# A hybrid decoder block on one core: transposed operands of the two attention groups built by VectorE and a trip through DRAM instead of by TensorE

## The chip, the cores and the metric

The kernel runs on one core of one Trainium2 chip. The metric is the device time of one execution in microseconds (us); three runs were made. Besides them there is one profiled execution, from which all rows below come. A core has five engines with queues of their own: TensorE (PE, matmuls, results go to PSUM), VectorE (DVE), ScalarE (ACT), GpSimd (POOL) and SyncE (SP), which here issues nearly all DMAs. Engines wait for each other through semaphores, and each engine works through its instructions strictly in the order in which they are written.

## The reference

256 tokens of 1024 numbers pass through one block. After an RMS norm, a projection `h @ w_in` gives the parts of two head groups.

```python
b = cumsum(log_a) in chunks of 64            # GLA: gated linear attention, 4 heads, dk 64, dv 128
q_dec, k_inv = q * exp(b), k * exp(-b)
a = where(causal, q_dec @ k_inv.T, 0)        # per head
o = a @ v + q_dec @ state                    # state carried over the chunks
# MoBA: 4 heads of 128; 256 tokens are one block, so it is plain causal attention
p = softmax(rotary(mq) @ rotary(mk).T * dh**-0.5, causal)
o_moba = p @ mv
```

Each head's output is RMS-normed (GLA also gated by silu(gr)), both groups go through `w_out` onto the residual x, and a SwiGLU of width 2816 and a last norm follow. All is float32.

## The kernel before

Every float32 product with a weight is built from three matmuls: weights and activations are split into a rounded high part and the low rest, and hi x hi, hi x lo and lo x hi are summed in PSUM (`product`, L471 to L473). Weights come in units of 128x2048 numbers (1 MB). SP loads unit u into one of three `raw` buffers when VectorE is done with unit u-3 (`raw_free`). ScalarE casts it to `w_hi` (`split`, L858), VectorE subtracts to get `w_lo` (its `split`, L1072), and six buffers of both feed TensorE. Units 0 to 11 are w_in in blocks of 512 columns, two units a block, in the order gla q and k, moba q, moba k, moba v, gla v, gla gate; units 12 to 15 are w_out; then eleven FFN phases of three units each. ScalarE takes a finished block out of PSUM with `take_block(b, ...)` (L875).

The small steps of the two attention groups are put between these units by hand. On TensorE the tables `midway` (after a unit's first token tile) and `after` (behind a unit) say where; on the other engines the order of the program does it. The steps touched are:

- GLA: VectorE scales q and k by the decays (L1180 to L1185). `gla_transposed`, behind unit 4, turns ten 128x128 tiles by matmuls with the identity (L576); ScalarE and VectorE copy them into `qdT`, `kiT`, `qcT`. `gla_scores` (L626) stands behind unit 6. `qdT` holds the query rows of the two heads of a pair apart; each scores matmul uses the 64 rows of one head.
- MoBA: `rotate(0)` and `rotate(1)` on VectorE (L1170 to L1175) apply the rotary embedding to queries and keys. `moba_transposed(0)`, behind unit 6, and `moba_transposed(1)`, in the middle of unit 7, turn eight tiles each; copies go to `mT` (L935, L940 on ScalarE, L1194, L1208 on VectorE). `moba_scores` (L636, L640) stands behind unit 7. VectorE adds the mask and takes the row maxima (L1212 to L1222), ScalarE the exponentials (L948). `probs_transposed`, in the middle of unit 9, turns twelve tiles, copied out by L955 and L1227. `moba_outputs` (L658) and `gla_updates` (L670) stand in the middle of unit 10; in the middle of unit 11 stand `heads_transposed(0)` and then `gla_outputs` (L682, L685).

The transposes of VectorE itself work in blocks of 32x32 inside a group of 32 partitions. The FFN phases already use them: sixteen instructions of 32x128 numbers per phase (L1321).

Of the kernel before, what the change touches and what calls it, by code (L numbers as in the profile page):

```python
# [22 lines left out]
P = 128  # L23
SEQ, D = 256, 1024
T = SEQ // P
KC = D // P
HEADS = 4
DV = 128
DK = 64
# [25 lines left out]
QUADS = 4  # L55
# [34 lines left out]
def build_block(nc, x, positions, norm1_gain, w_in, w_gate_up, b_gate, gla_out_gain, moba_out_gain,  # L90
# [6 lines left out]
    with ExitStack() as ctx:  # L97
# [83 lines left out]
        k_end, q_cum = (reuse_c[:, 1024 + QK * i:1024 + QK * (i + 1)] for i in range(2))  # L181
# [11 lines left out]
        mT = reuse_f[:, :].rearrange("p (w h s) -> p w h s", w=2, h=HEADS)  # L193
# [60 lines left out]
        glaT_in_psum = sem("glaT_in_psum")  # L254
        glaT_by_act = sem("glaT_by_act")
        glaT_by_dve = sem("glaT_by_dve")
        mT_in_psum = sem("mT_in_psum")
        mT_by_act = sem("mT_by_act")
        mT_by_dve = sem("mT_by_dve")
# [42 lines left out]
        out1_right_ready = sem("out1_right_ready")  # L302

# [4 lines left out]
        def _(sp):  # L308
# [84 lines left out]
        def _(pool):  # L393
# [14 lines left out]
            nc.gpsimd.memset(qdT[:, :, :, :], 0.0)  # L408
# [58 lines left out]
        def _(pe):  # L467
# [118 lines left out]
            def cumulate():  # L586
# [5 lines left out]
                for t, tri in enumerate((tri_rest, tri_cum)):  # L592
                    cols = slice(t * QK, (t + 1) * QK)
                    nc.tensor.matmul(aux[:, 3, cols], tri[:, :], log_hi[:, cols], start=True, stop=False)
                    last = nc.tensor.matmul(aux[:, 3, cols], tri[:, :], log_lo[:, cols], start=False, stop=True)
                last.then_inc(cum_in_psum, 1)

            def gla_transposed():
                pe.wait_ge(gla_ops_ready, 3)
                for bank, src in ((1, q_mid), (2, k_mid)):  # L600
                    transposes(bank, [src[:, t, pair * P:(pair + 1) * P] for pair in range(PAIRS)
                                      for t in range(T)]).then_inc(glaT_in_psum, 1)
                transposes(0, [q_cum[:, pair * P:(pair + 1) * P] for pair in range(PAIRS)]).then_inc(glaT_in_psum, 1)

            def moba_transposed(which):
                pe.wait_ge(rotated, which + 1)
                if which == 0:
                    pe.wait_ge(glaT_by_act, 3)
                else:
                    pe.wait_ge(mT_by_act, 1)  # L610
                    pe.wait_ge(mT_by_dve, 1)
                for n, bank in enumerate((3, 0)):
                    transposes(bank, [m_rot[:, which, t, h, :] for h in (2 * n, 2 * n + 1)
                                      for t in range(T)]).then_inc(mT_in_psum, 1)

            def gla_scores():

                pe.wait_ge(glaT_by_act, 2)
                pe.wait_ge(glaT_by_dve, 1)
                for t in range(T):  # L620
                    tok = slice(t * P, (t + 1) * P)
                    for pair in range(PAIRS):
                        col = (t * PAIRS + pair) * P
                        for par in range(2):
                            rows = slice(par * DK, (par + 1) * DK)
                            last = nc.tensor.matmul(aux[:, 1 + par, col:col + P], kiT[rows, pair, tok],  # L626
                                                    qdT[rows, pair, par, tok], start=True, stop=True)
# [782 lines left out]
```

## Time and profile before

| | us |
|---|---|
| median of 3 runs | 305.72 (305.68 to 305.84) |
| the profiled execution's own time | 305.38 |
| its span, first to last instruction | 303.7 |
| TensorE busy in it | 296.2 |
| VectorE busy | 231.7 |
| ScalarE busy | 153.7 |
| GpSimd busy | 21.9 |

The span is what the trace covers; the device time holds 1.7 us more around it. "Busy" sums the instructions of an engine. A matmul's duration is longer than its distance to the next one, since they are pipelined, so costs on TensorE are read from start to start. The granted clock is given as a share of full speed, the DMA share as the mean share of the core's 16 DMA engines that were moving data.

### The profile page before, as it was taken

The numbers are of one execution on the slowest core, as the hardware profiler recorded it, in microseconds if no ns is written. First come the engines' busy times: TensorE is split into PE (matmuls) and PEld (weight loads), VectorE is DVE, ScalarE is ACT, GpSimd is POOL, SyncE is SP. The second block draws the span as 40 slices with busy tenths as digits, with TensorE's granted clock in tenths as the row PEclk, the third lists the DMA queues.
The fourth block names the chain that finished last, engine by engine and source line by source line (L and its number), as shares of the span: only waits on it lengthen the run. The fifth ranks groups of instructions, "written<-read, shape, count | busy, mean of one in ns | idle before, by whom it ended". The sixth has DMA issues, their size and how long they took to land.

```text
span 303.7 us, 4006 instructions
## 1 busy us (share of the span) xinstructions
PE 296.2 (98%) x1407; PEld 247.1 (81%) x1407; DVE 231.7 (76%) x375; ACT 153.7 (51%) x189; POOL 21.9 (7%) x42
## 2 busy tenths in 40 slices
PE   8999999999999999999999999999999999999992
PEld 7788888888888888888888888888888888888881
DVE  1999999996487257679797979797878878787155
ACT  2898994699363527326262626262617071713123
POOL 6050100000112001500000000000000000000011
PEclk9999999999999999999999999999999999999998
DMA  7987856337825303914747474747472919030003
GB/s 233 359 294 254 276 200 218 138 141 276 276 86 192 138 2 92 316 77 156 262 158 259 159 255 158 256 163 252 139 276 82 331 34 368 19 133 0 0 2 138
DMA packets 36599, 54.42 MB, mean 179 GB/s; under 512 B 2870, under 2 KB 25962, under 8 KB 36586
## 3 DMA queue, kind: packets, MB, share of 16 engines
q1 hardware_dynamic: 36420, 54.08, 52.1%
q8 instruction: 8, 0.13, 0.2%
q10 hardware_dynamic: 166, 0.17, 0.2%
q14 instruction: 5, 0.04, 0.0%
HBM read 53.19 MB, written 1.05 MB: 179 GB/s over the span
## 4 chain that ended last, share of the span: by engine, by line
PE 94%; DMA 2%; DVE 1%; issue 1%; POOL 1%; ACT 0%; SPq 0%; POOLq 0%; DVEq 0%
PE acc L471 15%; PE acc L473 14%; PE acc L472 14%; PE aux L471 13%; PE aux L472 13%; PE aux L473 13%; PE aux L576 3%; DMA raw<-in_w_in 2%; PE acc L525 1%; PE acc L528 1%; PE acc L531 1%; PE aux L658 1%; DVE x_sb L1285 1%; PE aux L682 1%; PE aux L640 1%
## 5 line engine op out<-in xcount | busy, mean ns | idle before, releaser
L1072 DVE TENSOR_TENSOR w_lo<-raw,w_hi 128x2048 fp32r<-128x2048 f32 x47 | 105.6, 2287 | 11.3 <-ACT w_hi L858 11.2
L858 ACT CAST w_hi<-raw 128x2048 fp32r<-128x2048 f32 x47 | 87.7, 1907 | 6.9 <-DMA raw<-in_w_out 3.3
L471 PE MATMUL aux<-w_hi,aT_hi 128*128 128x512 f32 (+1 forms) x180 | 69.8, 388 | 0.0
L473 PE MATMUL aux<-w_hi,aT_lo 128*128 128x512 f32 (+1 forms) x180 | 69.6, 387 | 0.0
L472 PE MATMUL aux<-w_lo,aT_hi 128*128 128x512 f32 (+1 forms) x180 | 69.6, 387 | 0.0
L1321 DVE STREAM_TRANSPOSE reuse_c<-reuse_c 32x128 f32<-32x128 f32 x160 | 48.4, 303 | 2.4
L471 PE MATMUL acc<-w_hi,aT_hi 128*128 128x512 f32 x118 | 47.3, 401 | 0.0
L473 PE MATMUL acc<-w_hi,aT_lo 128*128 128x512 f32 x118 | 46.1, 391 | 0.0
L472 PE MATMUL acc<-w_lo,aT_hi 128*128 128x512 f32 x118 | 46.0, 390 | 0.0
L473 PEld LDWEIGHTS aux<-w_hi,aT_lo 128*128 128x128 f32 x180 | 33.8, 188 | 6.9
L471 PEld LDWEIGHTS aux<-w_hi,aT_hi 128*128 128x128 f32 x180 | 33.8, 188 | 6.9
L472 PEld LDWEIGHTS aux<-w_lo,aT_hi 128*128 128x128 f32 x180 | 33.8, 188 | 6.7
L1015 ACT CAST pT_hi<-reuse_c 128x512 fp32r<-128x512 f32 x10 | 6.2, 621 | 64.7 <-DVE reuse_c L1321 64.7
L471 PE MATMUL acc<-w_hi,pT_hi 128*128 128x512 f32 x80 | 31.2, 390 | 0.0
L473 PE MATMUL acc<-w_hi,pT_lo 128*128 128x512 f32 x80 | 31.1, 389 | 0.0
L472 PE MATMUL acc<-w_lo,pT_hi 128*128 128x512 f32 x80 | 31.1, 389 | 0.0
L1002 ACT ACTIVATE reuse_c<-aux,rstd 128x256 f32<-128x256 f32 x22 | 10.2, 472 | 32.4 <-PE aux L473 32.3
L473 PEld LDWEIGHTS acc<-w_hi,aT_lo 128*128 128x128 f32 x118 | 22.2, 188 | 4.8
L471 PEld LDWEIGHTS acc<-w_hi,aT_hi 128*128 128x128 f32 x118 | 22.2, 188 | 4.4 <-issue 0.2
L472 PEld LDWEIGHTS acc<-w_lo,aT_hi 128*128 128x128 f32 x118 | 22.2, 188 | 4.3
L1311 DVE SCALAR_TENSOR_TENSOR reuse_c<-aux,rstd,reuse_c 128x256 f32<-128x256 f32 x22 | 10.2, 480 | 13.2 <-ACT reuse_c L1002 13.2
L473 PEld LDWEIGHTS acc<-w_hi,pT_lo 128*128 128x128 f32 x80 | 15.0, 188 | 3.2
(199 smaller groups left out, 272.1 us busy)
## 6 DMA issues: line engine op xcount, KB each, us to landing
raw<-in_w_ffn_gate SPq DMA_DIRECT2D x22, 512.0 KB, 4.2
raw<-in_w_ffn_up SPq DMA_DIRECT2D x22, 512.0 KB, 5.3
raw<-in_w_ffn_down SPq DMA_DIRECT2D x22, 512.0 KB, 5.7
raw<-in_w_in SPq DMA_DIRECT2D x20, 512.0 KB, 4.7
raw<-in_w_out SPq DMA_DIRECT2D x8, 512.0 KB, 3.9
raw<-in_w_in SPq DMA_DIRECT2D x8, 256.0 KB, 6.2
x_sb<-in_x SPq DMA_DIRECT2D x2, 512.0 KB, 3.9
reuse_a<-in_final_norm_gain SPq DMA_DIRECT2D x1, 512.0 KB, 4.3
```

Source lines behind the costliest of these rows:

```text
L471: nc.tensor.matmul(dst, left_hi[:, k, tok], right_hi, start=first, stop=False)
L472: nc.tensor.matmul(dst, left_hi[:, k, tok], right_lo, start=False, stop=False)
L473: return nc.tensor.matmul(dst, left_lo[:, k, tok], right_hi, start=False, stop=last)
L525: nc.tensor.matmul(acc[:, t, :], aT_hi[:, k, toks[t]], right_hi, start=k == 0, stop=False)
L528: nc.tensor.matmul(acc[:, t, :], aT_hi[:, k, toks[t]], right_lo, start=False, stop=False)
L576: last = nc.tensor.transpose(aux[:, bank, n * P:(n + 1) * P], src, ident[:, :])
L858: nc.scalar.copy(w_hi[:, slot % RING, :], raw[:, slot % RAW, :]).then_inc(hi_ready, 1)
L1002: nc.scalar.activation(silu_g[:, t, :], aux[:, GATE_UP_BANKS[parity][t], 0:FF], ACT.Silu, scale=rstd[:, 1, t:t + 1]).then_inc(silu_ready, 1)
L1015: nc.scalar.copy(dst, src.rearrange("p (k s) -> p k s", k=2)).then_inc(hiddenT_hi_ready, 1)
L1072: nc.vector.tensor_tensor(w_lo[:, slot % RING, :], raw[:, slot % RAW, :], w_hi[:, slot % RING, :].bitcast(f32), ALU.subtract).then_inc(lo_ ...
L1311: nc.vector.scalar_tensor_tensor(out=hidden[:, t, :], in0=aux[:, GATE_UP_BANKS[parity][t], FF:2 * FF], scalar=rstd[:, 1, t:t + 1], in1=sil ...
L1321: last = nc.vector.transpose(cols[SQUARE * c:SQUARE * (c + 1), :, :, g, :], rows[SQUARE * g:SQUARE * (g + 1), :, :, c, :])
```

## The change

The ten GLA tiles and the sixteen MoBA tiles no longer pass through TensorE. VectorE turns all 32x32 blocks of a set of tiles in one wide instruction (`gla_squares`: 128x1280; `m_squares`: 128x1024 for the queries, the same for the keys). SP then stores each result in a DRAM scratch tensor (`squares_out`, one DMA) and reads it back so that every block lands in the right group of 32 partitions (`columns_back`, four DMAs of 32 partitions, after a wait until the store is done). ScalarE copies those parts that serve as stationary operands into a contiguous form (`kT`, 768 columns; `mT_q`, 1024 columns); the others are read by the matmuls as they land.

Moved with it: `moba_scores` from behind unit 7 to behind unit 8, `probs_transposed` from the middle of unit 9 to behind it, `gla_outputs` ahead of `heads_transposed(0)` and ScalarE's squares ahead of its copies of the head outputs. On ScalarE, split(9) goes behind take_block(2), split(12) behind the exponentials, take_block(3) ahead of split(11). On VectorE, rotate(1) goes ahead of split(8), split(9) behind the masked copies of the GLA scores, split(12) behind the copy of the probabilities. `q_cum` and `k_end` and the two halves of the PSUM bank of their decays change places, so that the ten tiles lie side by side. The memset of `qdT` goes.

```diff
-        qdT = sb("qdT", [PAIRS, 2, SEQ])
-        kiT = sb("kiT", [PAIRS, SEQ])
-        qcT = sb("qcT", [PAIRS, P])
+        gla_columns = sb("gla_columns", [QUADS, GLA_TILES, SQUARE])
+        kT = sb("kT", [3 * PAIRS, P])
...
+        gla_moves = nc.dram_tensor("gla_moves", (P, QUADS, GLA_TILES * SQUARE), f32).ap()
+        m_moves = [nc.dram_tensor(f"m_moves_{w}", (P, QUADS, MOBA_TILES * SQUARE), f32).ap() for w in "qk"]
...
-            for u in range(RAW, IN_UNITS):
-                raw_free(u)
-                rows_unit(u % RAW, w_in[0], (u % 2) * 4 * P, 4, BLOCKS[u // 2], 512)
+            def squares_out(ready, n, moves, squares, moved):
+                sp.wait_ge(ready, n)
+                sp.dma_start(moves, squares.rearrange("p c n i -> p c (n i)")).then_inc(moved, 16)
+
+            def columns_back(moved, moves, columns, landed):
+                sp.wait_ge(moved, 16)
+                for c in range(QUADS):
+                    sp.dma_start(columns[SQUARE * c:SQUARE * (c + 1)].rearrange("p g n i -> p g (n i)"),
+                                 moves[:, c, :].rearrange("(g j) n -> j g n", g=QUADS)).then_inc(landed, 16)
+
+            in_units(RAW, 9)
+            squares_out(gla_squares_ready, 1, gla_moves, gla_squares, gla_moved_out)
+            in_units(9, 10)
+            columns_back(gla_moved_out, gla_moves, gla_columns, gla_columns_back)
+            in_units(10, 11)
+            squares_out(m_squares_ready, 1, m_moves[0], m_squares[0], m_moved_out[0])
+            columns_back(m_moved_out[0], m_moves[0], m_columns[0], m_columns_back[0])
+            squares_out(m_squares_ready, 2, m_moves[1], m_squares[1], m_moved_out[1])
+            in_units(11, IN_UNITS)
+            columns_back(m_moved_out[1], m_moves[1], m_columns[1], m_columns_back[1])
...
             def gla_scores():
-                pe.wait_ge(glaT_by_act, 2)
-                pe.wait_ge(glaT_by_dve, 1)
+                pe.wait_ge(gla_columns_back, 16 * QUADS)
+                pe.wait_ge(kT_ready, 1)
...
             def moba_scores():
-                pe.wait_ge(mT_by_act, 2)
-                pe.wait_ge(mT_by_dve, 2)
+                pe.wait_ge(mT_q_ready, 1)
+                pe.wait_ge(m_columns_back[1], 16 * QUADS)
                 pe.wait_ge(a_ready, 2)
...
-            midway = {2: [logits], 7: [lambda: moba_transposed(1)],
-                      9: [probs_transposed], 10: [moba_outputs, gla_updates], 11: [lambda: heads_transposed(0, (3, 0)), gla_outputs]}
-            after = {3: [cumulate], 4: [gla_transposed],
-                     6: [gla_scores, lambda: moba_transposed(0)], 7: [moba_scores]}
+            midway = {2: [logits], 10: [moba_outputs, gla_updates], 11: [gla_outputs, lambda: heads_transposed(0, (3, 0))]}
+            after = {3: [cumulate], 6: [gla_scores], 8: [moba_scores], 9: [probs_transposed]}
...
             split(8)
-            act.wait_ge(glaT_in_psum, 1)
-            nc.scalar.copy(qdT[0:DK, :, 0, :], ...).then_inc(glaT_by_act, 1)
-            act.wait_ge(glaT_in_psum, 2)
-            nc.scalar.copy(kiT[:, :, :], ...).then_inc(glaT_by_act, 1)
-            act.wait_ge(glaT_in_psum, 3)
-            nc.scalar.copy(qcT[:, :, :], ...).then_inc(glaT_by_act, 1)
-            split(9)
             act.wait_ge(rotated, 1)
             take_block(2, m_flat)
-            act.wait_ge(mT_in_psum, 1)
-            nc.scalar.copy(mT[:, 0, 0:2, :], ...).then_inc(mT_by_act, 1)
+            split(9)
+            act.wait_ge(gla_columns_back, 16 * QUADS)
+            nc.scalar.copy(kT[...], gla_columns[...]).then_inc(kT_ready, 1)
             split(10)
+            act.wait_ge(m_columns_back[0], 16 * QUADS)
+            nc.scalar.copy(mT_q[...], m_columns[0][...]).then_inc(mT_q_ready, 1)
+            act.wait_ge(rotated, 2)
+            take_block(3, mv)
             split(11)
-            act.wait_ge(rotated, 2)
-            act.wait_ge(mT_in_psum, 3)
-            nc.scalar.copy(mT[:, 1, 0:2, :], ...).then_inc(mT_by_act, 1)
-            split(12)
-            take_block(3, mv)
...
             nc.scalar.preload_act_table(ACT.Silu)
+            split(12)
             split(13)
...
+            dve.wait_ge(gla_ops_ready, 3)
+            nc.vector.transpose(gla_squares, gla_rows).then_inc(gla_squares_ready, 1)
             split(6)
             split(7)
-            rotate(0)
+            for which in range(2):
+                rotate(which)
+                dve.wait_ge(rotated, which + 1)
+                nc.vector.transpose(m_squares[which], m_rows[:, which]).then_inc(m_squares_ready, 1)
             split(8)
-            dve.wait_ge(glaT_in_psum, 1)
-            nc.vector.tensor_copy(qdT[DK:P, :, 1, :], ...).then_inc(glaT_by_dve, 1)
-            rotate(1)
-            dve.wait_ge(mT_in_psum, 2)
-            nc.vector.tensor_copy(mT[:, 0, 2:4, :], ...).then_inc(mT_by_dve, 1)
-            split(9)
...
                 last.then_inc(a_ready, 1)
-            dve.wait_ge(mT_in_psum, 4)
-            nc.vector.tensor_copy(mT[:, 1, 2:4, :], ...).then_inc(mT_by_dve, 1)
+            split(9)
             split(10)
```

## Rows read from the trace of the kernel before

**Rows 1.** The page: busy us, share of the span, instructions; the chain that ended last.

```profile
PE 296.2 (98%) x1407; PEld 247.1 (81%) x1407; DVE 231.7 (76%) x375; ACT 153.7 (51%) x189; POOL 21.9 (7%) x42
...
PE 94%; DMA 2%; DVE 1%; issue 1%; POOL 1%; ACT 0%; SPq 0%; POOLq 0%; DVEq 0%
```

**Rows 2.** Stretches: busy us per engine (instructions), granted clock, DMA share, GB/s.

```profile
34.00:52.00 18.00, 18.00 (x90) 14.81 (x90) 17.36 (x24) 14.19 (x18) 0.96 (x1) 1.00 0.65 218
52.00:63.00 11.00, 11.00 (x72) 9.58 (x70) 10.11 (x14) 6.29 (x5) 0.00 (x0) 1.00 0.43 154
63.00:81.00 18.00, 18.00 (x105) 15.30 (x103) 11.86 (x10) 13.42 (x29) 0.00 (x0) 1.00 0.67 243
```

**Rows 3.** TensorE in order of time: start, duration, instruction; a run of one kind merged.

```profile
39.50 1.25 PE L576 MATMUL aux<-ident,reuse_c 128*128 128x128 f32 x10
40.51 0.48 PE L471 MATMUL acc<-w_hi,aT_hi 128*128 128x512 f32 x1
...
46.06 0.39 PE L471 MATMUL acc<-w_hi,aT_hi 128*128 128x512 f32 x1
...
51.27 0.39 PE L473 MATMUL acc<-w_hi,aT_lo 128*128 128x512 f32 x1
...
52.69 1.09 PE L576 MATMUL aux<-ident,reuse_e 128*128 128x128 f32 x8
53.53 0.48 PE L471 MATMUL acc<-w_hi,aT_hi 128*128 128x512 f32 x1
...
56.40 1.04 PE L576 MATMUL aux<-ident,reuse_e 128*128 128x128 f32 x8
57.19 0.48 PE L471 MATMUL acc<-w_hi,aT_hi 128*128 128x512 f32 x1
```

**Rows 4.** The same view: MoBA scores, the product behind them, MoBA outputs.

```profile
60.01 1.05 PE L636 MATMUL aux<-reuse_f 128*128 128x128 f32 x8
...
62.44 0.58 PE L471 MATMUL acc<-w_hi,aT_hi 128*128 128x512 f32 x1
...
77.61 2.84 PE L658 MATMUL aux<-mv,reuse_f 128*128 128x128 f32 x24
```

**Rows 5.** VectorE: a group of the page (busy, mean ns); then in order of time.

```profile
L1321 DVE STREAM_TRANSPOSE reuse_c<-reuse_c 32x128 f32<-32x128 f32 x160 | 48.4, 303 | 2.4
...
37.76 4.49 DVE L1072 TENSOR_TENSOR w_lo<-raw,w_hi 128x2048 fp32r<-128x2048 f32 x2
42.18 0.69 DVE L1170 TENSOR_TENSOR reuse_e<-reuse_d,cos_t 128x512 f32<-128x512 f32 x1
...
45.57 0.69 DVE L1175 TENSOR_TENSOR reuse_e<-reuse_e,mv 128x512 f32<-128x512 f32 x1
...
65.19 0.17 DVE L1222 TENSOR_SCALAR neg_max<-row_max 128x4 f32<-128x4 f32 x1
```

**Rows 6.** ScalarE in order of time; in brackets idle time before and what ended it.

```profile
47.40 1.26 ACT L875 ACTIVATE reuse_d<-acc,rstd 128x512 f32<-128x512 f32 x2
...
67.36 0.51 ACT L948 ACTIVATE reuse_e<-reuse_e,neg_max 128x256 f32<-128x256 f32 x1
67.77 0.19 ACT L948 ACTIVATION_READ_ACCUMULATOR reuse_e<-reuse_e,neg_max 128x1 f32 x1
...
69.27 1.91 ACT L858 CAST w_hi<-raw 128x2048 fp32r<-128x2048 f32 x1
71.47 1.08 ACT L955 COPY reuse_f<-aux 128x512 f32<-128x512 f32 x2 [0.29 <-PE aux L576]
```

**Rows 7.** DMA issues: count, KB, us from issue to landing; then SP's queue in time.

```profile
raw<-in_w_ffn_gate SPq DMA_DIRECT2D x22, 512.0 KB, 4.2
...
out<-reuse_e SPq DMA_DIRECT2D x2, 256.0 KB, 2.2
...
40.08 0.88 SPq L320 DMA_DIRECT2D raw<-in_w_in  x2
```

**Rows 8.** Stretch at the end, TensorE: busy us, granted clock, DMA share, GB/s.

```profile
290.00:303.70 13.70, 7.69 (x40) 0.93 0.21 78
```

More of the change, by code:

```diff
@@ L180, in build_block @@
         q_mid, k_mid = (reuse_c[:, 512 * i:512 * i + 512].rearrange("p (t n) -> p t n", t=T) for i in range(2))
-        k_end, q_cum = (reuse_c[:, 1024 + QK * i:1024 + QK * (i + 1)] for i in range(2))
+        q_cum, k_end = (reuse_c[:, 1024 + QK * i:1024 + QK * (i + 1)] for i in range(2))
+        gla_rows = reuse_c[:, 0:GLA_TILES * P].rearrange("p (n c i) -> p c n i", c=QUADS, i=SQUARE)
+        gla_squares = reuse_f[:, 0:GLA_TILES * P].rearrange("p (c n i) -> p c n i", c=QUADS, i=SQUARE)
         squares = reuse_c[:, 0:1024]
@@ L192, in build_block @@
         s_1 = reuse_e[:, 512:1536].rearrange("p (h k) -> p h k", h=HEADS)
-        mT = reuse_f[:, :].rearrange("p (w h s) -> p w h s", w=2, h=HEADS)
+        m_columns = [reuse_f[:, 1024 * w:1024 * (w + 1)].rearrange("p (c n i) -> p c n i", c=QUADS, i=SQUARE) for w in range(2)]
+        mT_q = reuse_a[:, :].rearrange("p (t h s) -> p t h s", t=T, h=HEADS)
+        mT_k = reuse_f[:, 1024:2048].rearrange("p (c t h i) -> p t h c i", c=QUADS, t=T, h=HEADS)
+        m_rows = reuse_e[:, :].rearrange("p (w n c i) -> p w c n i", w=2, c=QUADS, i=SQUARE)
+        m_squares = [buf.rearrange("p (c n i) -> p c n i", c=QUADS, i=SQUARE)
+                     for buf in (reuse_a[:, :], reuse_c[:, 0:1024])]
         probT = reuse_f[:, 0:1536].rearrange("p (b h q) -> p b h q", b=3, h=HEADS)
@@ L253, in build_block @@
         gla_ops_ready = sem("gla_ops_ready")
[L254 to L259, printed above, removed]
+        gla_squares_ready = sem("gla_squares_ready")
+        gla_moved_out = sem("gla_moved_out")
+        gla_columns_back = sem("gla_columns_back")
+        kT_ready = sem("kT_ready")
+        m_squares_ready = sem("m_squares_ready")
+        m_moved_out = [sem(f"m_moved_out_{w}") for w in "qk"]
+        m_columns_back = [sem(f"m_columns_back_{w}") for w in "qk"]
+        mT_q_ready = sem("mT_q_ready")
         a_zeroed = sem("a_zeroed")
@@ L592, in cumulate @@
                 for t, tri in enumerate((tri_rest, tri_cum)):
-                    cols = slice(t * QK, (t + 1) * QK)
-                    nc.tensor.matmul(aux[:, 3, cols], tri[:, :], log_hi[:, cols], start=True, stop=False)
-                    last = nc.tensor.matmul(aux[:, 3, cols], tri[:, :], log_lo[:, cols], start=False, stop=True)
+                    cols, dst = slice(t * QK, (t + 1) * QK), slice((1 - t) * QK, (2 - t) * QK)
+                    nc.tensor.matmul(aux[:, 3, dst], tri[:, :], log_hi[:, cols], start=True, stop=False)
+                    last = nc.tensor.matmul(aux[:, 3, dst], tri[:, :], log_lo[:, cols], start=False, stop=True)
                 last.then_inc(cum_in_psum, 1)
[L598 to L614, printed above, removed]
             def gla_scores():
-                pe.wait_ge(glaT_by_act, 2)
-                pe.wait_ge(glaT_by_dve, 1)
+                pe.wait_ge(gla_columns_back, 16 * QUADS)
+                pe.wait_ge(kT_ready, 1)
                 for t in range(T):
-                    tok = slice(t * P, (t + 1) * P)
                     for pair in range(PAIRS):
@@ L639, in moba_scores @@
                 for h in range(HEADS):
-                    last = nc.tensor.matmul(aux[:, 2 + h // 2, (h % 2) * SEQ:(h % 2 + 1) * SEQ], mT[:, 0, h, P:SEQ],
-                                            mT[:, 1, h, :], start=True, stop=True)
+                    last = nc.tensor.matmul(aux[:, 2 + h // 2, (h % 2) * SEQ:(h % 2 + 1) * SEQ], mT_q[:, 1, h, :],
+                                            mT_k[:, :, h, :, :], start=True, stop=True)
                     if h % 2:
```

34 lines of the change are left out of this document (18 added, 16 removed).

## The prediction

> **What bounds the kernel now.** I read the page first: TensorE is busy for 98% of the span and is 94% of the chain that ended last [rows 1]. Next I read busy time by stretch: from 34 to 81 us, where most of the change lies, TensorE has no free time at all and its clock is at full speed; up to 63 us VectorE is close behind it, with 17.4 of 18 and 10.1 of 11 us [rows 2]. So the kernel is a queue of matmuls. What leaves this queue is gained in full, and what makes it wait is lost in full. The third view was TensorE in order of time [rows 3, 4], then the other engines at the points where the new order ties TensorE to them [rows 5 to 7].
>
> **What is removed.** Three groups of transposes leave TensorE. By starts, the ten GLA transposes take 39.50 to 40.51 us, and the product behind them lasts 0.48 instead of 0.39 us: 1.01 + 0.09 = 1.1 us. The query group takes 52.69 to 53.53, 0.84 us; the slow restart behind it stays, since the GLA scores now stand there. The key group takes 56.40 to 57.19, and with its restart 0.88 us [rows 3]. Sum: **-2.85 us**, an upper bound of the gain. The copies of their results out of PSUM leave ScalarE and VectorE; those engines are followed below.
>
> **First wait, GLA scores.** A unit of weights is 24 products, from 46.06 to 51.27 + 0.23 = 5.44 us [rows 3]. Without the ten transposes units 5 and 6 end at 39.50 + 10.9 = 50.4, and the scores now need a ScalarE copy (kT_ready). Its chain: VectorE's added transpose of 1280 columns. One of 128 columns takes 0.303 us, a 128x512 pass 0.69, so 128 more columns cost about 0.13, and 1280 cost 0.303 + 9 x 0.13 = 1.5 us, of which some 0.07 overlaps its neighbour. It stands before split(6), so the first rotation, ready at 45.57 + 0.69 = 46.26 before, is ready at 47.7 [rows 5]. The profile shows no such wide transpose. Lower bound 0.83 us (a pass with one source at twice the speed), upper bound 2 us (ten at 0.303 less overlaps); I take 1.45, since both rows it lies between run at this rate. Behind the rotation ScalarE runs take_block(2), 1.26, split(9), 1.91 [rows 6], and the kT copy of 768 columns, about 0.8 (half as much again as a 512-column copy at 0.54). Less overlaps of 0.1 each that is 51.7. TensorE waits 51.7 - 50.4 = **1.3 us**. Behind the waiting scores stands everything else on TensorE. The other input, the moved columns, is not later by my estimate: VectorE is done at 39.2, the store lands near 43.2, the return is issued from 43.2 to 45.0 behind unit 9 and lands near 49 (bounds 47.5 and 51).
>
> **The moves.** Nothing in the trace goes through DRAM and back. The nearest rows: a 256 KB store lands 2.2 us after issue, a 512 KB load of 1 KB rows 4.2 us, an issue costs 0.44 us on SP [rows 7]. So I take about 3.4 us for each store of 512 or 640 KB and, for four returns issued 0.45 apart, 4.2 us from the first issue. The stretch 34 to 52 moved 218 GB/s at a DMA share of 0.65, so about 330 GB/s when busy [rows 2]; a weight unit of 1 MB then holds the engines 3.1 us. SP's queue in order: unit 9 at 41.5, GLA return 43.2, unit 10 at 45.0, query store when VectorE has turned them. That is 47.7 + 1.24 = 49.0 and behind unit 10's bytes, landed 53.7; query return issued to 55.5, landed 57.9. The keys are turned at 54.4 (second rotation 4.1 us, then 1.24), but SP is free only at 55.5; their store lands at 59.4. Unit 11 goes in between, at 56.7, when split(8) is done, and the key return, issued from 59.4, has its bytes behind it: it lands at **64.6**. Bounds: 61.8 if no transfer is held by another, 67.4 if each return needs a further 1 to 1.5 us and every queue delay falls on this chain.
> Every unit behind keeps its slack: split(8) at 56.7 against TensorE's unit 8 at 58.4, split(9) at 60.2 against 66, split(10) at 62.4 against 74.
>
> **Second wait, scores.** After the first wait GLA scores take 1.2 us and units 7 and 8 10.9, so TensorE comes to the MoBA scores at 63.8. The wait is 64.6 - 63.8 = **0.8 us**, bounds 0 and 3.6. Call the start of these scores S; before it was 60.01 [rows 4].
>
> **Third wait, MoBA outputs.** Before, with S = 60.01, the second maxima end at 65.19 + 0.17 = S + 5.35, the exponentials at 67.77 + 0.19 = S + 7.95, after take_block(3) had held the first four back; without this, four of 0.41 + 0.19 us, each overlapped by 0.1, behind the maxima give S + 7.4 [rows 5, 6]. TensorE: scores 2.43, a unit 5.44 and restarts, so the probability transposes start at S + 8.05: not late, by 0.6 us only. They take 1.3 (twelve at 0.10, as in rows 3, and a restart), half a unit 2.72: TensorE wants the transposed probabilities at S + 12.1. ScalarE has a table load until S + 8.75 (1.3, from 67.96 to 69.27), then split(12) and split(13), 1.83 each, where only one stood before, then two copies, 1.08 [rows 6]: S + 13.5. Wait **1.4 us**. Then the outputs, 2.77 [rows 4], to S + 16.3, while split(14) and take_block(4) end at S + 16.5: **0.2 us** more for the GLA updates. If those two splits stood behind the copies, 1.4 would be nothing.
>
> **The rest.** After these steps TensorE stands at the middle of unit 11 at S + 22.7. The swap of GLA outputs and head transposes puts ScalarE's squares before its copies; headsT is ready about 4.1 us after this point, wanted at 6.3: hidden. The later order of split(12) on VectorE is hidden by more than 10 us of lead. The memset of qdT that GpSimd drops, the swapped halves of the decay bank and the new shapes of the score operands (same count and columns) I put at nothing: bounds +-0.1. Four restarts out of a wait, of some 0.07 each: **0.3 us** (bounds 0 and 0.6).
>
> **Sum:** -2.85 + 1.3 + 0.8 + 1.4 + 0.2 + 0.3 = **+1.15 us**. The profiled execution took 305.38 us for its span of 303.7, which is 0.34 below the median of 305.72; 305.38 + 1.15 = 306.5 would be its like, and against the median the forecast is **306.9 us**.
>
> **A rule weighed.** The key return's chain rests on row 7's 2.2 us for 256 KB. The Trainium skill, "DMA: Bandwidth & Descriptors", section on the anatomy of one DMA, gives about 2.0 us fixed plus bytes over 436 GB/s, most of the fixed part being the receipt of the write, heaviest for HBM; the 2.2 us is a little below its 2.6. By it alone store and return would be about 3.2 us each and the key columns would be there before S, an estimate that leaves out the weights in front. The sum would be about 0.8 lower. It is the first rival's case.
>
> **Rivals.** (1) *No DMA wait*: the key columns land by 63.8. For it: the bound of 61.8, and a DMA share of 0.43 from 52 to 63 us [rows 2]. Against: SP, in order, holds unit 11 between. The sum is then +0.35, 306.1. (2) *The move chain is the bound*: the key columns land at 66 to 67.4, or the GLA columns later than ScalarE. For it: two round trips in series on one queue and 3.4 MB on top of the weights. The key wait is 2.2 to 3.6, the time 308.3 to 309.7. (3) *Faster*: VectorE's wide transposes run like a pass with one source, 0.83 and 0.68 us. Then the rotation comes 0.65 earlier, the first wait is 0.65, the key chain gains more than 1 us and its wait goes; with restarts at nothing -2.85 + 0.65 + 1.6 = -0.6, 305.1. It decides at a wide transpose of 0.9 us or less. Against: 303 ns for 128 columns. (4) *The clock falls*: TensorE now has idle gaps of 1 us or more close together. In the last stretch, where it is idle for 6.0 of 13.7 us, the granted clock shows 0.93, in the stretches without idle time 1.00 [rows 2, 8]. If it fell to the lower level of 1.2 GHz after the third wait, half a unit of 2.7 us would take 5.4: +3 to +5 us on the sum, 309.9 to 311.9.
> The Trainium skill, "TensorE: Matmul & The Clock Gate", says that an engine that has been idle is put back to half clock until it has again been busy; whether the gaps forecast here would do it, nothing in the trace shows.
>
> **How the numbers follow.** Forecast, key wait between 0.3 and 2: 0.45. (1) 0.25, (2) 0.16, (3) 0.10, (4) 0.04. What a measurement can tell from no change is about 0.2%, 0.6 us. Slower by more: nearly all of the forecast's case, (2), (4) and a little of (1): 0.66. Within: 0.24. Faster: 0.10. The range 305.2 to 309.3 leaves out half of (3), a part of (2) and (4); the forecast's own is 306.3 to 308.2.
>
> **What would show it.** TensorE's list has no 128x128 products out of ident between 39 and 57 us; the GLA scores wait about 1.3 us for ScalarE's kT; the MoBA scores wait for a DMA by about 0.8; the MoBA outputs wait about 1.4 us for ScalarE's copy of the probabilities. A wide transpose lasts 1.5 and 1.24 us. The stretches behind 110 us are unchanged. I am wrong if TensorE meets the MoBA outputs without a wait, or if a store or return lands more than 1.5 us away from the times given.

## The result and the profile after

| | before | after |
|---|---|---|
| median of 4 runs, us | 305.78 (305.68 to 306.10) | 309.12 (308.48 to 311.54) |
| ratio to before | | 1.0131, 95% interval 1.0101 to 1.0162 |
| the profiled execution's own time, its span | 305.38, 303.7 | 311.54, 309.8 |

The changed kernel is 1.3% slower: +3.34 us in the medians, against +1.15 in the forecast. The direction was right and the time lies at the upper end of the range, among the times of rival (2), though the keys landed later than that rival has them. The profiled execution of after is the slowest of its four, so it shows +6.1 us of span; the experiments below hold a second profile of the same kernel with +5.0. No profile shows an execution at the median, so there the waits below must be shorter than in either.

The page of after: busy us, share and instructions; the chain that ended last; then its DMA issues with the median us to landing.

```profile
PE 296.0 (96%) x1381; PEld 246.5 (80%) x1381; DVE 233.9 (76%) x375; ACT 153.1 (49%) x186; POOL 21.1 (7%) x41
...
PE 82%; ACT 5%; DVE 5%; issue 3%; DMA 2%; SPq 1%; POOL 1%; POOLq 0%; DVEq 0%; ACTq 0%
...
gla_columns<-gla_moves SPq DMA_DIRECT2D x4, 160.0 KB, 6.0
m_moves_q<-reuse_a SPq DMA_DIRECT2D x1, 512.0 KB, 6.0
...
m_moves_k<-reuse_c SPq DMA_DIRECT2D x1, 512.0 KB, 3.7
reuse_f<-m_moves_k SPq DMA_DIRECT2D x4, 128.0 KB, 4.0
```

TensorE issues 26 matmuls fewer and yet is busy for about as long as before [rows 1]: about half of what the transposes cost has gone into slower score matmuls, 1.44 us as shown below. Its share of the chain fell from 94% to 82%; the other engines and DMA now stand in it. TensorE in order of time at the three places where it waits (start, duration, in brackets the idle time ahead of it and what ended it); these answer to [rows 3, 4]. The first row is the last product ahead of the GLA scores:

```profile
50.52 0.39 PE L507 MATMUL acc<-w_hi,aT_lo 128*128 128x512 f32 x1
52.63 1.16 PE L642 MATMUL aux<-gla_columns,kT 64*128 64x128 f32 x16 [1.73 <-ACT kT L943]
...
69.00 2.05 PE L652 MATMUL aux<-reuse_f,reuse_a 128*128 128x128 f32 x8 [4.10 <-issue]
...
72.87 0.58 PE L505 MATMUL acc<-w_hi,aT_hi 128*128 128x512 f32 x1
...
83.56 2.94 PE L674 MATMUL aux<-mv,reuse_f 128*128 128x128 f32 x24 [0.77 <-ACT reuse_f L965]
```

The books of this execution, by starts: -2.85 (transposes) + 1.79 (first wait: the scores start 2.11 behind the last product, before 0.32) + 4.25 (MoBA scores wait for the keys) + 1.44 (these scores take 3.87 instead of 2.43) + 0.92 (wait at the outputs) + 0.20 (the outputs themselves take 2.97 instead of 2.77) + 0.38, by which the whole queue stands later already at the cumulate step, ahead of the change (33.47 against 33.09). That makes 6.13, and the spans differ by 6.1. Nothing later adds to it. Stretches (busy us per engine, granted clock, DMA share, GB/s):

```profile
58.00:62.00 4.00, 4.00 (x19) 3.33 (x18) 4.00 (x3) 2.21 (x3) 0.00 (x0) 1.00 1.03 338
62.00:66.00 4.00, 2.91 (x13) 2.06 (x11) 0.58 (x1) 0.00 (x0) 0.00 (x0) 1.00 1.10 266
66.00:70.00 4.00, 1.00 (x5) 1.03 (x6) 0.00 (x0) 1.90 (x1) 0.00 (x0) 0.80 1.02 376
70.00:74.00 4.00, 4.00 (x18) 3.49 (x18) 2.81 (x6) 1.26 (x7) 0.00 (x0) 0.77 0.24 96
```

Two things stand here that before did not have: from 58 to 70 us the DMA engines have no free time (shares of 1.0 and above; before, 0.43 from 52 to 63 [rows 2]), and the clock falls in the stretches at 66 and 70, behind the long gap. SP's queue (start, us spent issuing) says what stands in front of what; ScalarE and VectorE below say when the data came:

```profile
42.76 2.09 SPq L383 DMA_DIRECT2D gla_columns<-gla_moves  x4
44.90 0.94 SPq L333 DMA_DIRECT2D raw<-in_w_in  x2
...
55.30 1.75 SPq L383 DMA_DIRECT2D reuse_f<-m_moves_q  x4
57.09 0.43 SPq L378 DMA_DIRECT2D m_moves_k<-reuse_c  x1
57.57 1.35 SPq L333 DMA_DIRECT2D raw<-in_w_in  x2
60.84 1.75 SPq L383 DMA_DIRECT2D reuse_f<-m_moves_k  x4
```

ScalarE, with what ended its idle time in brackets:

```profile
51.66 0.83 ACT L943 COPY kT<-gla_columns 128x768 f32<-128x768 f32 x1 [0.57 <-DMA gla_columns<-gla_moves]
54.04 1.92 ACT L872 CAST w_hi<-raw 128x2048 fp32r<-128x2048 f32 x1 [1.55 <-DMA raw<-in_w_in]
...
66.39 1.90 ACT L872 CAST w_hi<-raw 128x2048 fp32r<-128x2048 f32 x1 [4.57 <-DMA raw<-in_w_in]
```

VectorE's wide transposes:

```profile
38.13 1.51 DVE L1197 STREAM_TRANSPOSE reuse_f<-reuse_c 128x1280 f32<-128x1280 f32 x1
...
53.43 1.25 DVE L1203 STREAM_TRANSPOSE reuse_c<-reuse_e 128x1024 f32<-128x1024 f32 x1
```

The key chain reads: turned at 54.68 (53.43 + 1.25), but SP waits for the query store, issued at 49.30, until 55.30 and issues the query return to 57.05; store 57.09 to about 60.8; unit 11 issued in between, landed at 66.39, 8.8 us later; return issued from 60.84 on, and TensorE starts at 69.00. "issue" in its bracket is only what the profile calls a wait with no releaser in sight; the longest of the four pieces of this return took 6.7 us, and issued last, at 62.2, it lands just before 69.0. Unit 10 took 9.1 us (44.9 to 54.04). Single weight issues, 30 to 80 us of before:

```profile
DMA to landing us min/median/max: 3.3/4.2/5.7
```

The same from 36 to 82 us of after:

```profile
DMA to landing us min/median/max: 3.3/6.9/9.7
```

### The profile page after: what moved, and what is told of

Same layout as the page of the kernel before. It is cut to its first block, busy times and chain, and to the rows that moved or that the text cites. A ratio compares the mean times of both kernels' runs of the same rounds, so it can differ in the third digit from the quotient of the medians.

```text
span 309.8 us, 3962 instructions
## 1 busy us (share of the span) xinstructions
PE 296.0 (96%) x1381; PEld 246.5 (80%) x1381; DVE 233.9 (76%) x375; ACT 153.1 (49%) x186; POOL 21.1 (7%) x41
## 4 chain that ended last, share of the span: by engine, by line
PE 82%; ACT 5%; DVE 5%; issue 3%; DMA 2%; SPq 1%; POOL 1%; POOLq 0%; DVEq 0%; ACTq 0%
PE aux L507 13%; PE aux L506 13%; PE aux L505 13%; PE acc L505 11%; PE acc L507 11%; PE acc L506 11%; DMA gla_columns<-gla_moves 2%; ACT w_hi L872 2%; PE acc L522 1%; PE aux L610 1%; PE acc L559 1%; PE acc L562 1%; PE acc L565 1%; PE aux L674 1%; PE aux L531 1%
## 5 line engine op out<-in xcount | busy, mean ns | idle before, releaser
L506 PEld LDWEIGHTS acc<-w_lo,pT_hi 128*128 128x128 f32 x80 | 15.0, 188 | 3.1
```

The lines of the kernel that those rows point to most:

```text
L506: nc.tensor.matmul(dst, left_hi[:, k, tok], right_lo, start=False, stop=False)
```

## Experiments

My theory was: the loss is the key chain through DRAM, whose transfers hold each other up behind weight units on one queue, plus the clock. The rivals were: the new order of the engines' work itself, the width of the queue, and w_out's loads. Each run is compared with the kernel before on the same chip.

**The order without the trips.** `e1_no_moves`: SP issues weights only, the matmuls read VectorE's blocks where they lie.

```diff
-        gla_squares = reuse_f[:, 0:GLA_TILES * P].rearrange(...)
+        gla_squares = gla_columns[:, :, :, :]
-        m_squares = [... (reuse_a[:, :], reuse_c[:, 0:1024])]
+        m_squares = m_columns
...
-            act.wait_ge(gla_columns_back, 16 * QUADS)
+            act.wait_ge(gla_squares_ready, 1)
```

> Leaves out the DRAM trips: VectorE turns its blocks straight into the buffers that the scores read, so the blocks stay in their old partition groups and the scores are not the reference's; order and all other instructions as in the changed kernel. Theory (the moves' lateness is the loss): the long wait at the MoBA scores (4.2 us in the changed kernel's trace) and the low clock behind it (scores 3.9 instead of 2.4 us) go; the first wait stays at about 1.3 us (ScalarE's take_block(2), split(9), kT copy behind the rotation), the wait at the MoBA outputs is 1.4. Sum about -2.85+1.3+1.4+0.2+0.2 = +0.2: 305.7 to 306.3 us. Rival (the order on ScalarE and VectorE costs by itself as much as the transposes gave, moves or not): 308 or more. Rival (the waits are all the moves' doing): 303.5 or less.

Measured 305.57 us, ratio 0.9997 (0.9986 to 1.0008). TensorE of this run:

```profile
52.03 1.16 PE L632 MATMUL aux<-gla_columns,kT 64*128 64x128 f32 x16 [1.08 <-ACT kT L933]
...
77.66 2.94 PE L664 MATMUL aux<-mv,reuse_f 128*128 128x128 f32 x24 [1.17 <-ACT reuse_f L955]
```

ScalarE's two waits, 1.08 and 1.17, are there without any DMA, the MoBA scores start at 64.14 without one, and with the restarts they eat the 2.85 us of the transposes. The whole of the +3.3 is therefore DMA and what it brings.

**Unit 11 behind the key return.** `e2_keys_first`:

```diff
-            in_units(11, IN_UNITS)
             columns_back(m_moved_out[1], m_moves[1], m_columns[1], m_columns_back[1])
+            in_units(11, IN_UNITS)
```

> The key return is issued ahead of unit 11 on SP. Theory (the return comes late since 1 MB of weights is ahead of it in SP's queue): keys land about 3 us sooner, near 65.5 to 66 us, the wait at the scores falls from 4.2 to about 1 us, no low clock: 306 to 307 us. Rival (the trip itself, store then return, is slow whatever stands ahead): store from 57.1, landed 60.8, return to 65 at the least, but the units issued right behind slow its last part again: wait still 3 to 4 us, 308.5 or more. Side effect to watch: unit 11 lands later, and ScalarE's split(11) stands ahead of the exponentials.

Measured 307.58 us, 1.0055 (1.0038 to 1.0072). Its key return:

```profile
reuse_f<-m_moves_k SPq DMA_DIRECT2D x4, 128.0 KB, 2.8
```

TensorE of the same run:

```profile
65.38 1.13 PE L652 MATMUL aux<-reuse_f,reuse_a 128*128 128x128 f32 x8
...
74.11 1.53 PE L610 MATMUL aux<-ident,reuse_e 128*128 128x128 f32 x12 [0.39 <-ACT reuse_e L957]
...
80.09 2.94 PE L674 MATMUL aux<-mv,reuse_f 128*128 128x128 f32 x24 [1.72 <-ACT reuse_f L965]
```

With 1 MB less in front the return takes 2.8 us instead of 4.0, the scores start at 65.38 and take 2.5 us at full clock, and 1.4 us come back in the medians (2.3 by the ratios). Part is given back: unit 11 comes later, ScalarE's split(11) waited 6.4 us for it, and both later steps wait longer. The query store still takes 6.2 us behind unit 10. The profiled execution has a mean granted clock of 0.996 over its span; the other three have 0.989, so in them the clock may have fallen somewhere after all.

**The moves on a queue of their own.** `e3_gpsimd_queue`:

```diff
-                sp.wait_ge(ready, n)
-                sp.dma_start(moves, ...)
...
+                pool.wait_ge(ready, n)
+                pool.dma_start(moves, ...)
```

> Stores and returns are issued by GpSimd, which has nothing to do there; SP issues only weights. Theory (waiting in SP's in-order queue is the loss): query store at 49.3 is not behind unit 10 and unit 11 is not held; key store starts at 54.7, not at 57.1; keys land by 63, no wait at the scores, GLA columns land by 47: total 305.8 to 306.5. Rival (the 16 DMA engines are the limit, their share is 0.9 to 1.0 from 58 to 70 us): key columns land within 1.5 us of the changed kernel's 69 and the time stays at 308 to 309.5.

Measured 317.38 us, 1.0368 (1.0339 to 1.0398). Its DMA issues:

```profile
gla_columns<-gla_moves POOLq DMA_DIRECT2D x4, 160.0 KB, 7.1
...
m_moves_k<-reuse_c POOLq DMA_DIRECT2D x1, 512.0 KB, 9.0
```

The stretch of its first wait (clock 0.64):

```profile
50.00:58.00 8.00, 4.22 (x22) 3.45 (x22) 7.83 (x11) 3.13 (x3) 2.51 (x5) 0.64 0.59 161
```

TensorE:

```profile
53.97 2.08 PE L638 MATMUL aux<-gla_columns,kT 64*128 64x128 f32 x16 [3.78 <-ACT kT L939]
...
74.22 2.05 PE L648 MATMUL aux<-reuse_f,reuse_a 128*128 128x128 f32 x8 [5.64 <-issue]
```

A miss: the idea that SP's order was the trouble and a free queue its cure fell. Weights are no longer held back by SP's waits and are in flight together with every move. The returns take 4.9 to 7.1 us, the key store 9.0, both waits grow (3.78 and 5.64) and the clock falls behind both. What is short is mainly the transfer time of the 16 engines, whose share is 0.99 or more from 58 to 70 us; SP's order decides only who gets it first. A small part is the other way of issuing: the GLA store, issued onto free engines, took 3.5 us from GpSimd and 2.9 from SP.

**ScalarE: the probabilities' copies first.** `e4_probs_first` puts the copies of L965 ahead of split(12) and split(13).

```diff
-            split(12)
-            split(13)
...
             nc.scalar.copy(probT[...], aux[...])
+            split(12)
+            split(13)
```

> ScalarE copies the transposed probabilities before split(12) and split(13). Theory (the third wait is ScalarE's order): the wait of 0.8 to 1.4 us at the MoBA outputs goes, and that of 0.2 at the GLA updates may grow by little; 0.8 to 1.4 us less than the changed kernel: about 308.0. Rival (other work sets that wait too): less than 0.4 us less.

Measured 311.49 us, 1.0215 (1.0160 to 1.0269): not faster than the change. TensorE:

```profile
67.15 2.05 PE L652 MATMUL aux<-reuse_f,reuse_a 128*128 128x128 f32 x8 [2.41 <-issue]
...
85.27 0.66 PE L686 MATMUL aux<-gv,reuse_c 128*64 128x128 f32 x8 [1.42 <-ACT gv L889]
```

The outputs start at 81.01 without a wait; the wait stands 24 matmuls later, now 1.42 us for take_block(4), because three splits (5.5 us) are still ahead of that. The prediction's sentence that the 1.4 us "would be nothing" behind such a swap was wrong: the wait is for ScalarE's whole queue. The four runs spread over 3.7 us, the widest here. The two longer ones (312.63 and 314.00) ran at a mean granted clock of 0.987 and 0.986, the two shorter at 0.990 and 0.991, the four of the change at 0.991 to 0.996. So the lower clock goes with the higher median; what brought it about is not shown.

**w_out's loads held back.** `e5_hold_w_out`, beside a second run of the change itself.

```diff
             columns_back(m_moved_out[1], m_moves[1], m_columns[1], m_columns_back[1])
+            sp.wait_ge(m_columns_back[1], 16 * QUADS)
```

> The order of the changed kernel, but SP issues units 12 and on only when the key return has landed. Theory A (the end of the key return is late because two more units, 2 MB, are issued 0.4 us behind it and share the 16 DMA engines): the last of its four DMAs, 6.7 us in the changed kernel's trace, lands in 4 us or less, the scores start about 2 us sooner (67 instead of 69), the clock stays up, 1.5 to 3 us less than the change: near 307. Theory B (unit 11 ahead of it is the cause): scores again near 68 to 69, same time as the change.

> The change unaltered, on the chip of these runs: 308.5 to 311.5 us, with wait at the MoBA scores of 2 to 4.5 us, a lower clock while they run, and about 0.8 us at the MoBA outputs. It is the yardstick for what the other kernels of this series change and for the copy-probabilities-first kernel (311.49), whose trace had no wait at the MoBA outputs but 1.4 us at the GLA updates. If the change too comes to 310.5 or more here, that kernel is no slower than it.

Measured: held back 308.54 us, 1.0083 (1.0063 to 1.0103); the change again (`e6_change_again`) 309.90 us, 1.0139 (1.0103 to 1.0175). TensorE with w_out's loads held back:

```profile
67.46 1.13 PE L653 MATMUL aux<-reuse_f,reuse_a 128*128 128x128 f32 x8 [2.07 <-issue]
```

This lies between theories A and B. SP issues w_out's first load at 67.38, when the key return has landed, so the scores do wait for this return. Its longest piece takes 4.6 us, where it took 5.4 in the change again, 4.9 in `e4_probs_first`, whose DMA order is the change's, and 6.7 in after. From the return's first issue to the scores it is 6.0 us, against 6.8, 6.4 and 8.2. With unit 11 behind the return, in `e2_keys_first`, it is 4.4. So unit 11 ahead of the return costs 1.7 us or more, and w_out's loads behind it seem to cost something too, 0.3 to 2.1 us on the longest piece by these single profiles. In the medians holding them back gave 1.4 us; the intervals touch, so how much it is worth stays open. TensorE of the second run of the change:

```profile
64.34 0.39 PE L507 MATMUL acc<-w_hi,aT_lo 128*128 128x512 f32 x1
67.73 1.13 PE L652 MATMUL aux<-reuse_f,reuse_a 128*128 128x128 f32 x8 [3.00 <-issue]
...
71.52 0.97 PE L505 MATMUL acc<-w_hi,aT_hi 128*128 128x512 f32 x1
```

The same picture with a shorter key wait: by starts 3.16 us, the scores 3.79 instead of 2.43, and the first wait 1.53, the third 0.75. So the key wait differs by over 1 us between two executions of one kernel.

**Both orders mended at once.** `e7_keys_first_act_order` is `e2_keys_first` with, on ScalarE, take_block(4) and the copies ahead of split(12) to split(14).

```diff
-            split(12)
-            split(13)
+            take_block(4, gv)
...
             nc.scalar.copy(probT[...], aux[...])
+            split(12)
+            split(13)
             split(14)
-            take_block(4, gv)
```

> Key return ahead of unit 11 (307.58 alone, with 1.7 us of wait at the MoBA outputs and 0.2 at the GLA updates) and on ScalarE take_block(4) and the probability copies ahead of split(12) to split(14). Theory (these waits are ScalarE's chain of table load, two splits, copies, split, take_block(4)): both waits go, 1.9 us less: 305.7. Rival (as when only the copies were moved: the wait turns up further down, at the GLA updates, the head transposes or a late weight unit): 306.5 or more.

Measured 308.17 us, 1.0082 (1.0060 to 1.0105). TensorE:

```profile
52.23 1.16 PE L642 MATMUL aux<-gla_columns,kT 64*128 64x128 f32 x16 [1.68 <-ACT kT L943]
...
87.96 1.35 PE L698 MATMUL aux<-gv,reuse_b 128*128 128x128 f32 x10 [0.73 <-DVE state L1261]
```

The stretch around the first wait (clock 0.79):

```profile
50.00:58.00 8.00, 6.33 (x33) 4.83 (x32) 7.86 (x12) 3.49 (x3) 0.00 (x0) 0.79 0.72 227
```

The scores (65.95), outputs (78.14) and updates no longer wait. In their place the clock fell behind the first wait, and VectorE's split(12) to split(14), which wait for ScalarE's casts, made its `state` late for the GLA outputs; another 0.75 us is lost at the out product (95.25). The expected 305.7 did not come; the rival, waits that turn up further down, did.

**Every order at once.** `e8_all_orders` puts the GLA return ahead of unit 9, the query store ahead of unit 10, the key return ahead of unit 11, kT ahead of split(9), take_block(4) and the copies ahead of splits 11 and 12, and the later splits of VectorE likewise.

```diff
             in_units(RAW, 9)
             squares_out(gla_squares_ready, 1, gla_moves, gla_squares, gla_moved_out)
-            in_units(9, 10)
             columns_back(gla_moved_out, gla_moves, gla_columns, gla_columns_back)
-            in_units(10, 11)
+            in_units(9, 10)
             squares_out(m_squares_ready, 1, m_moves[0], m_squares[0], m_moved_out[0])
+            in_units(10, 11)
...
-            split(9)
             nc.scalar.copy(kT[...], gla_columns[...])
+            split(9)
```

> All moves kept, every order round them changed: GLA return ahead of unit 9, query store ahead of unit 10, key return ahead of unit 11; kT copy ahead of split(9); split(11) and later behind the probabilities on ScalarE and VectorE. Theory (all of the loss is order, none is inherent): kT ready at about 50.1 us instead of 52.6, key columns before 62.5, no wait at the MoBA outputs: most of the 2.85 us of the transposes is gained, 303.0 to 303.8. Rival (the 3.4 MB of traffic itself delays weights or keys): a wait of 1 us or more remains at the scores or at a unit of weights, 304.5 or more.

Measured 314.73 us, 1.0289 (1.0264 to 1.0315). TensorE:

```profile
65.32 1.13 PE L652 MATMUL aux<-reuse_f,reuse_a 128*128 128x128 f32 x8 [2.03 <-issue]
...
100.00 0.76 PE L505 MATMUL acc<-w_hi,aT_hi 128*128 128x512 f32 x1 [7.00 <-ACT aT_hi L978]
```

The GLA scores start at 51.01 without a wait, with kT begun at 49.39. But the whole is far slower, from a wait I had not foreseen: ScalarE's head copies stood behind split(16), whose weights came late (4.94 us of waiting for DMA), and TensorE lost 7.00 us at the out product. `e11_orders_mended` puts that right:

```diff
-            split(16)
             take_headsT(0)
+            split(16)
```

> All orders changed as in the kernel that came to 314.7, with ScalarE's split(16) behind its copies of the MoBA heads. Theory (of that kernel's loss 7.0 us was one wait: the head copies stood behind split(16), whose weights came late): this wait goes, the wait of 2 us for the key columns stays, all other waits stay away: 305.0 to 306.3. Rival (weights really come too late once the splits are moved): a wait at an out-product, 307 or more.

Measured 307.51 us, 1.0061 (1.0042 to 1.0079). TensorE:

```profile
64.47 1.13 PE L652 MATMUL aux<-reuse_f,reuse_a 128*128 128x128 f32 x8 [2.31 <-issue]
65.44 3.46 PE L656 MATMUL aux<-reuse_f,reuse_a 128*128 128x256 f32 x8
...
107.37 0.47 PE L505 MATMUL acc<-w_hi,aT_hi 128*128 128x512 f32 x1 [1.38 <-DVE aT_lo L1086]
```

The stretch behind the second wait:

```profile
66.00:74.00 8.00, 8.00 (x30) 6.50 (x30) 3.94 (x7) 4.51 (x17) 0.00 (x0) 0.81 0.71 282
```

The GLA scores start at 49.89 without a wait. The key store takes 5.8 us and the return is issued at 60.11. What the GLA step wins, TensorE arrives earlier at the scores and waits there: with the key return ahead of unit 11 the scores start at 64.5 to 66.0 us in all four runs that have this order, and here TensorE could be there at 62.2. The rival came in part as well: 1.38 us are lost at the out product. The clock fell in the profiled execution (0.991 over its span); the other three have 0.996 and 0.997 and are 0.5 to 1.2 us shorter.

**The price of a transpose.** `e9_fewer_transposes` is the kernel before with one tile per group turned, 7 of 26; which part of the output that touches, the expectation says.

```diff
-                    transposes(bank, [m_rot[:, which, t, h, :] for h in (2 * n, 2 * n + 1)
-                                      for t in range(T)]).then_inc(mT_in_psum, 1)
+                    transposes(bank, [m_rot[:, which, 0, 2 * n, :]]).then_inc(mT_in_psum, 1)
```

> The kernel before with only 7 of its 26 transposes of GLA and MoBA operands on TensorE (one per group; the other tiles are left out, so the scores are not the reference's); every copy, wait and order stays. Theory (TensorE's queue is the bound, each transpose costs its 0.10 us in full): 19 x 0.10 = 1.9 us less, 303.8 us, so the change's -2.85 is real. Rival (part of it was hidden, by VectorE's lo halves or the weights): 304.8 or more.

Measured 304.08 us, 0.9951 (0.9933 to 0.9968): -1.5 by the ratio, 19 tiles x 0.10 = -1.9 expected. The size holds roughly, and -2.85 for all 26 is rather too much than too little, as the prediction said with "upper bound".

**The GLA part alone.** `e10_gla_only`: the kernel before, with the GLA tiles through DRAM, the return ahead of unit 9 and kT ahead of split(9); MoBA as before.

```diff
-            after = {3: [cumulate], 4: [gla_transposed],
+            after = {3: [cumulate],
...
+            in_units(RAW, 9)
+            squares_out(gla_squares_ready, 1, gla_moves, gla_squares, gla_moved_out)
+            columns_back(gla_moved_out, gla_moves, gla_columns, gla_columns_back)
+            in_units(9, IN_UNITS)
```

> Only the GLA tiles go by VectorE and DRAM, their return ahead of unit 9 and the kT copy ahead of split(9); MoBA as before. Gain 1.1 us of transposes; kT ready at about 50.0, TensorE comes at 50.4: no wait there. VectorE is 0.7 us later than before at the key copies while TensorE wants them 1.1 us sooner. Theory (order, not traffic, decides): a wait of 0 to 0.8 at the MoBA scores, 304.6 to 305.5. Rival (any trip through DRAM beside the weights loses more than ten transposes cost): 306 or more.

Measured 304.39 us, 0.9974 (0.9959 to 0.9989), with no wait of TensorE from 34 to 125 us. TensorE:

```profile
51.00 1.16 PE L637 MATMUL aux<-gla_columns,kT 64*128 64x128 f32 x16
```

The issue of the return:

```profile
gla_columns<-gla_moves SPq DMA_DIRECT2D x4, 160.0 KB, 3.6
```

The return takes 3.6 us with no unit in front of it, where in the change it took 6.0. One trip through DRAM pays, by a little, if nothing stands in its way and eleven microseconds (39.8 to 51.0) lie between the turned blocks and their use.

**A version that beats both.** `e12_keys_on_pe`: GLA tiles and queries through DRAM, the keys turned by TensorE in the middle of unit 7. The order of SP and the place of kT are those of `e11_orders_mended`; split(11) and the splits behind it come one step earlier on ScalarE and VectorE, so it is not that kernel with a single edit.

```diff
-            squares_out(m_squares_ready, 2, m_moves[1], m_squares[1], m_moved_out[1])
-            in_units(11, IN_UNITS)
-            columns_back(m_moved_out[1], m_moves[1], m_columns[1], m_columns_back[1])
+            in_units(11, IN_UNITS)
...
+            def keys_transposed():
+                pe.wait_ge(rotated, 2)
+                for n, bank in enumerate((3, 0)):
+                    transposes(bank, [m_rot[:, 1, t, h, :] for h in (2 * n, 2 * n + 1)
+                                      for t in range(T)]).then_inc(mT_in_psum, 1)
...
-            midway = {2: [logits], 10: ...
+            midway = {2: [logits], 7: [keys_transposed], 10: ...
```

> GLA tiles and queries go through DRAM, the keys are turned by TensorE as before (0.88 us of the 2.85 stay); the orders round them as in the mended kernel. Theory (the third trip in series is what cannot be hidden): no wait for GLA columns (kT at 50), queries back by 60, scores at 62.6: 303.6 to 304.4, faster than both kernels. Rival (the DMA engines are full from 50 to 66 us, so the queries come late as well): wait of 1 us or more at the scores, 305 or more.

Measured 303.66 us, 0.9936 (0.9919 to 0.9953): 0.6% faster than before. TensorE:

```profile
51.05 1.16 PE L649 MATMUL aux<-gla_columns,kT 64*128 64x128 f32 x16
...
64.06 1.05 PE L660 MATMUL aux<-reuse_f,reuse_a 128*128 128x128 f32 x8
```

The stretch of its busiest DMA:

```profile
58.00:66.00 8.00, 8.00 (x41) 6.85 (x40) 5.41 (x5) 6.03 (x5) 0.00 (x0) 1.00 1.04 337
```

No row of TensorE has a bracket from 34 to 125 us, and the clock shows 1.00 in every stretch from 42 to 100 us, though the DMA share from 58 to 66 is as high as in the change. For the 0.9 us of key transposes that it keeps, it has one round trip less, no wait at the scores and no fall of the clock. The Trainium skill, "VectorE: DVE Perf Modes", section "Rules for kernel authors", advises TensorE for a full 128x128 transpose where PSUM will do; for the keys, whose matmuls follow within ten microseconds, these runs agree (1.0061 against 0.9936, of which 2.31 us is the key wait of `e11_orders_mended`; its 1.38 us at the out product may belong to the other order of splits); for the GLA tiles they don't: there the way round was the faster one (0.9974).

## Why the prediction was right in sign and short in size

- **Transposes, -2.85.** Held, as a number rather too large than too small: 19 of the 26 left out brought 1.5 of the 1.9 us reckoned for them (`e9_fewer_transposes`).
- **First wait, 1.3.** 1.79 by starts in the profile of after, 1.53 in the second, 1.15 without the moves. The wide transpose was priced rightly, 1.51 us against 1.5. Wrong was the half sentence that "the moved columns" are not the later input: they landed at 51.66, not 49, since the return took 6.0 us behind unit 9. It cost the 0.57 in ScalarE's bracket.
- **Second wait, 0.8: the step that failed.** It measured 4.25 and 3.16 us. TensorE came at 64.75 (forecast 63.8), the last key piece near 69 (64.6) and near 67.7. The links: query store landed 55.3 for 53.7, key store 60.8 for 59.4, and from its first issue the return took 8.2 us, 6.8 in the second profile, where the forecast has 5.2 (59.4 to 64.6). So about 1.5 us of the lateness is there when the return is issued, and 1.6 to 3.0 come with unit 11 ahead of it and w_out's loads behind it. I had priced each transfer by rows in which it runs nearly alone, had added little for the bytes in front, and put the rest of the queueing in a bound that was itself too low: 67.4. The weight rows alone could have said more: three round trips put 3.4 MB on engines that were at a share of 0.65 and 0.43 [rows 2]. In after the single weight issues took 6.9 us in the median where they had taken 4.2. The sign of being wrong that the prediction names was there as well: the query store landed 1.6 us, the GLA return 2.7 and the key return 4.4 behind the times given. The Trainium skill's 2.0 us plus bytes over 436 GB/s ("DMA: Bandwidth & Descriptors", section "Anatomy of one DMA"), a fit for transfers that GpSimd issues, would give an estimate of 3.2 us for 512 KB; the two MoBA stores of that size, issued by SP, took 6.0 and 3.7 here. Its section "Rules for kernel authors" says that spreading transfers over several issuing engines gains no bandwidth; `e3_gpsimd_queue`, at a DMA share of 1.02 from 42 to 50 us, agrees.
- **The clock, rival (4).** The mechanism came, at another place: not behind the third wait, but behind the second. The granted clock is 0.80 and 0.77 from 66 to 74 us, a mixture of the levels of 2.4 and 1.2 GHz, and it cost 1.4 us. Here it is a consequence of the second wait: without that the clock stays at 1.00 in the profiles of `e1_no_moves` and `e2_keys_first`, and the mean over the span is 0.994 to 0.999 in all ten executions of `e1_no_moves`. For `e2_keys_first` only the profiled execution shows it. Other waits can do it too: in `e7_keys_first_act_order` the clock fell behind the first. It is the second part of the missing size.
- **Third wait 1.4, updates 0.2.** 0.92 (idle 0.77) and 0.20. Shorter than forecast, which fits that slow scores give ScalarE time; with scores at full speed `e1_no_moves` has 1.17 and `e2_keys_first` 1.72. The 0.20 has the forecast's size by luck: the updates have no wait for take_block(4). The outputs take 2.97 us up to the updates wherever they start out of a wait (after, `e1_no_moves`, `e2_keys_first`, `e6_change_again`) and 2.77 where they don't (before, `e11_orders_mended`, `e12_keys_on_pe`).
- **Rest.** Nothing behind 90 us differs, as stated.
- **Rival (2).** That its time, 308.3 to 309.7, holds the median is partly luck: its key columns land at 66 to 67.4 and it has no clock term, while in both profiles they landed later and the clock fell, and both profiled executions (311.54 and 310.39) are above its times.

In the median: the order alone comes to nothing (`e1_no_moves`), as forecast by -2.85 + 1.3 + 1.4 + 0.2 + 0.3 = +0.35; the DMA terms are the whole +3.3 where I had 0.8.

## What to carry to other kernels

A round trip through DRAM is not priced by the duration of its transfers when they run alone, but by what lies ahead of them on the queue and by the free transfer time in that stretch; count the bytes of the stretch before and after, and look at what is issued behind it too. Move off the bottleneck engine only what has a slack of one loaded round trip, 10 to 14 us here, and keep on it the operand that is needed soonest. When an order is changed to remove one wait, look for the next consumer of the same engine's queue: in three of these runs the wait only moved.

## What the runs showed of the hardware

- A wide 32x32 transpose on VectorE runs at 1.51 us for 128x1280 and 1.25 us for 128x1024 float32, 1.2 ns a column, while one of 32x128 takes 0.303.
- TensorE's clock behind its gaps. Seven gaps of 2.3 to 7.0 us (`e11_orders_mended` 2.31, `e4_probs_first` 2.41, `e6_change_again` 3.00, `e3_gpsimd_queue` 3.78 and 5.64, after 4.10, `e8_all_orders` 7.00) all have a fall of the clock at their end or behind them: by stretches of 4 us the lowest granted clock is 0.50 to 0.77. Of thirteen gaps of 1.0 to 2.1 us two have one, 0.61 and 0.74 (`e7_keys_first_act_order` 1.68, `e5_hold_w_out` 2.07); a gap of 2.08 in that same run and one of 2.03 in `e8_all_orders` left it at 1.00. What decides between equal gaps the runs don't show.
- The four DMAs of the same 640 KB return took a median of 3.5 to 3.6 us in front of a weight unit, 5.8 to 6.0 behind one, and 7.1 from GpSimd's queue beside SP's. A queue of its own did not make the moves faster.
